# The shared rotary key of an encoder layer: which operand stands still in TensorE and which one streams

## The reference, cut to what matters

```python
h = rms_norm(x, norm_mix_g[l])
z = h @ w_in[l]
u_conv, c_q, c_kv, k_pe, gate_logits = jnp.split(z, IN_SPLITS, axis=-1)   # k_pe: 64 columns
...
k_pe = apply_rope(k_pe, cos, sin)
k_full = jnp.concatenate(
    [k_nope, jnp.broadcast_to(k_pe[:, :, None, :], (B, S, MLA_HEADS, QK_ROPE))], axis=-1)
```

## Time and profile before

| | |
|---|---|
| median of the runs | 1637.82 us |
| the profiled execution, whole | 1639.63 us |
| its span, first to last instruction | 1637.8 us |
| TensorE busy with matmuls | 1624.3 us (99%), 7612 matmuls |
| TensorE busy with weight loads | 1360.0 us (83%) |
| VectorE / ScalarE / GpSimd busy | 1088.9 / 811.2 / 98.2 us |
| mean granted TensorE clock | 0.998 of 2.4 GHz |

### The profile page before, as it was taken

How to read it: one execution, slowest core, us unless ns; L and a number is a source line. 1 busy time by engine, 2 the same in 40 slices (tenths; PEclk the granted TensorE clock), 3 DMA queues, 4 the chain that set the end, 5 groups by cost and what they waited for, 6 DMA issues and landing times.

```text
span 1637.8 us, 22071 instructions
## 1 busy us (share of the span) xinstructions
PE 1624.3 (99%) x7612; PEld 1360.0 (83%) x7612; DVE 1088.9 (66%) x1480; ACT 811.2 (50%) x1062; POOL 98.2 (6%) x187
## 2 busy tenths in 40 slices
PE   9999999999999999999999999999999999999998
PEld 7888888888888888888889888888888888888886
DVE  5588888888888998656556655555555555545554
ACT  6444456555555556744445644334443444334443
POOL 6500010211111000000000000000000000000000
PEclk9999999999999999999999999999999999999999
DMA  7766655555555665557554566566656665566654
GB/s 242 204 191 187 186 160 162 173 170 175 180 166 160 219 201 184 183 190 249 199 186 150 166 182 190 192 193 182 192 189 192 193 182 186 193 191 186 190 188 138
DMA packets 160992, 304.78 MB, mean 186 GB/s; under 512 B 11657, under 2 KB 19969, under 8 KB 160513
## 3 DMA queue, kind: packets, MB, share of 16 engines
q1 hardware_dynamic: 159552, 299.41, 59.7%
q0 software_dynamic: 1056, 3.46, 0.6%
q10 hardware_dynamic: 320, 1.06, 0.2%
HBM read 301.78 MB, written 2.10 MB: 186 GB/s over the span
## 4 chain that ended last, share of the span: by engine, by line
PE 97%; ACT 1%; DVE 1%; DMA 0%; issue 0%; SPq 0%
PE ps L1328 30%; PE ps L1330 30%; PE ps L1329 30%; PE ps L1341 2%; PE ps L1512 1%; PE ps L1511 1%; PE ps L1601 0%; PE ps L1599 0%; PE ps L1600 0%; ACT hconv L759 0%; PE ps L1528 0%; DMA x_in<-in_x_dram 0%; PE ps L1522 0%; PE ps L1365 0%; PE ps L1692 0%
## 5 line engine op out<-in xcount | busy, mean ns | idle before, releaser
L895 DVE TENSOR_TENSOR wlo<-raw,whi 128x1024 fp32r<-128x1024 f32 x560 | 686.0, 1228 | 406.6 <-ACT whi L544 402.0
L544 ACT ACTIVATE whi<-raw 128x1024 fp32r<-128x1024 f32 x560 | 591.7, 1060 | 567.4 <-PE ps L1330 555.9
L1328 PE MATMUL ps<-whi,a_hi 128*128 128x512 f32 x1212 | 478.0, 394 | 0.0
L1330 PE MATMUL ps<-whi,a_lo 128*128 128x512 f32 x1212 | 472.3, 390 | 0.0
L1329 PE MATMUL ps<-wlo,a_hi 128*128 128x512 f32 x1212 | 471.9, 389 | 0.0
L1328 PE MATMUL ps<-whi,c_hi 128*128 128x512 f32 x752 | 293.8, 391 | 0.0
L1330 PE MATMUL ps<-whi,c_lo 128*128 128x512 f32 x752 | 292.7, 389 | 0.0
L1329 PE MATMUL ps<-wlo,c_hi 128*128 128x512 f32 x752 | 292.6, 389 | 0.0
L1330 PEld LDWEIGHTS ps<-whi,a_lo 128*128 128x128 f32 x1212 | 227.5, 188 | 47.8
L1329 PEld LDWEIGHTS ps<-wlo,a_hi 128*128 128x128 f32 x1212 | 227.7, 188 | 45.7
L1328 PEld LDWEIGHTS ps<-whi,a_hi 128*128 128x128 f32 x1212 | 227.6, 188 | 45.7 <-DVE wlo L895 0.2
(11 more groups left out here) (255 smaller groups left out, 1169.3 us busy)
## 6 DMA issues: line engine op xcount, KB each, us to landing
raw<-in_w_ff_dram SPq DMA_DIRECT2D x256, 512.0 KB, 4.0
raw<-in_w_in_dram SPq DMA_DIRECT2D x144, 512.0 KB, 3.7
raw<-in_w_mla_out_dram SPq DMA_DIRECT2D x32, 512.0 KB, 4.4
raw<-in_w_conv_out_dram SPq DMA_DIRECT2D x32, 512.0 KB, 4.2
raw<-in_w_out_dram SPq DMA_DIRECT2D x32, 512.0 KB, 4.6
raw<-in_w_ukv_dram SPq DMA_DIRECT2D x16, 512.0 KB, 3.7
raw<-in_w_xkv_dram SPq DMA_DIRECT2D x16, 512.0 KB, 4.1
raw<-in_w_uq_dram SPq DMA_DIRECT2D x16, 384.0 KB, 3.7
```

The source lines that it names most:

```text
L544: act.activation(whi[:, s, :], raw[:, s, :], ACT.Copy).then_inc(hi_ready, 1)
L895: dve.tensor_tensor(wlo[:, s, :], raw[:, s, :], whi[:, s, :].bitcast(F32), ALU.subtract).then_inc(lo_ready, 1)
L1328: pe.matmul(sum_, x_hi[:, k0 + k, tok], w_hi, start=(first and k == 0), stop=False)
L1330: mm = pe.matmul(sum_, x_lo[:, k0 + k, tok], w_hi, start=False, stop=(last and k == kts - 1))
```

## The change

The 128-token blocks of the activations stand, and the 64 weight columns move. There are 16 blocks of channels x 2 token halves x 3 products = 96 matmuls. Token rows come out at once, 128 tokens x 64 channels in bank 4 for the first half of the tokens and in bank 5 for the second. ScalarE reads `kpe_row` directly from these banks, with the same scale. The copy into `kpe_sum`, the two transposes, the tile and the semaphore `kpe_out` are gone, and the wait for `vec_ready` stands ahead of the matmuls.

```diff
# ScalarE
                 if k == 0:
                     act.wait_ge(used, U_KPE + 1)
-                    act.activation(kpe_sum[:], ps[0:ROPE, 4, 0:SEQ], ACT.Copy).then_inc(kpe_out, 1)
-                if k == 1:
-                    act.wait_ge(kpe_turned, 1)
                     for t in range(TT):
-                        last = act.activation(kpe_row[:, t, :], ps[:, 5, ROPE * t:ROPE * (t + 1)], ACT.Copy, scale=rs_x[:, t:t + 1])
+                        last = act.activation(kpe_row[:, t, :], ps[:, 4 + t, 0:ROPE], ACT.Copy, scale=rs_x[:, t:t + 1])
                     last.then_inc(kpe_ready, 1)
...
                 if k == 5:
-                    act.wait_ge(kpe_turned, 2)
+                    act.wait_ge(kpe_turned, 1)
# TensorE
             pe.wait_ge(lo_ready, U_KPE + 1)
+            pe.wait_ge(vec_ready, 2)
             s = U_KPE % RING
             for k in range(KT):
                 w_hi, w_lo = (w[:, s, ROPE * k:ROPE * (k + 1)] for w in (whi, wlo))
-                pe.matmul(ps[0:ROPE, 4, 0:SEQ], w_hi, a_hi[:, k, :], start=(k == 0), stop=False)
-                pe.matmul(ps[0:ROPE, 4, 0:SEQ], w_lo, a_hi[:, k, :], start=False, stop=False)
-                mm = pe.matmul(ps[0:ROPE, 4, 0:SEQ], w_hi, a_lo[:, k, :], start=False, stop=(k == KT - 1))
+                for t in range(TT):
+                    to, tok = ps[:, 4 + t, 0:ROPE], slice(P * t, P * (t + 1))
+                    pe.matmul(to, a_hi[:, k, tok], w_hi, start=(k == 0), stop=False)
+                    pe.matmul(to, a_hi[:, k, tok], w_lo, start=False, stop=False)
+                    mm = pe.matmul(to, a_lo[:, k, tok], w_hi, start=False, stop=(k == KT - 1))
             mm.then_inc(used, 1)
             for k in range(UPC):
                 unit(U_CKV + k, 0, a_hi, a_lo, 2 * k, 0, k == 0, k == UPC - 1)
-                if k == 0:
-                    pe.wait_ge(kpe_out, 1)
-                    pe.wait_ge(vec_ready, 2)
-                    for t in range(TT):
-                        tr = pe.transpose(ps[:, 5, ROPE * t:ROPE * (t + 1)], kpe_sum[:, P * t:P * (t + 1)], ident[0:ROPE, 0:ROPE])
-                    tr.then_inc(kpe_turned, 1)
```

More of the change, by code:

```diff
@@ L233, in build @@
         mask = at(o + 27648, "mask", [P, SW])
-        kpe_sum = at(o + 20480, "kpe_sum", [ROPE, SEQ])
         kpe_row = at(o + 29184, "kpe_row", [P, TT, ROPE])
@@ L313, in build @@
         ln_root, ln_scaled, silu_done, st_hi, st_lo = (sem(n) for n in ("ln_root", "ln_scaled", "silu_done", "st_hi", "st_lo"))
-        kpe_out, kpe_ready, kpe_prod, kpe_rotated, kpe_turned, kpeT_ready = (sem(n) for n in ("kpe_out", "kpe_ready", "kpe_prod", "kpe_rotated", "kpe_turned", "kpeT_ready"))
+        kpe_ready, kpe_prod, kpe_rotated, kpe_turned, kpeT_ready = (sem(n) for n in ("kpe_ready", "kpe_prod", "kpe_rotated", "kpe_turned", "kpeT_ready"))
         q_ready, qn_ready, kv_ready, q_prod, q_rotated = (sem(n) for n in ("q_ready", "qn_ready", "kv_ready", "q_prod", "q_rotated"))
```

## The result

The changed kernel takes 1652.99 us, the median of 4 runs (1652.17 to 1654.65), beside 1638.2 us for the kernel before (1637.47 to 1638.91, now 4 runs, one more than the 1637.82 rests on). The ratio is 1.0089 with a 95% interval of 1.0077 to 1.0101: slower by 14.8 us, where +5.1 (1642.9 us) was forecast. The profiled execution took 1652.17 us, 12.5 more than the one before.

A forecast was written before the change was run, and what follows sets the result against it. TensorE's own work was taken to bound the kernel (busy 1624.3 of 1637.8 us). +5.6 us for the rotary matmuls and -0.46 for the transposes gave +5.1, so 1642.9 us; own range 1642.0 to 1643.8, overall 1641.0 to 1652.5.

The forecast's parts named there:

- The likeliest case: Rotary matmuls load-bound at full clock, stretch 10.6 to 11.5 us, kernel about 5.1 us slower; chance 0.53.
- 96 x 0.115 = 11.0 us: Rotary stretch on TensorE: 96 new matmuls at 0.115 us each, against 5.45 us before, so +5.6 us.
- Rival A: Clock falls in the stretch of short rotary matmuls: +10.8 to +14.4 us, 1648.6 to 1652.2; chance 0.26.
- higher case: Clock falls 3.6 us into the rotary stretch, 65 matmuls at 0.23 us follow: +14.4 us, 1652.2.
- The row behind its 0.23 us: Trace row giving (2.50 - 0.42)/9 = 0.23 us for a 128-column load and pass, taken as the lower-clock price.
- the one stretch that lost its clock: Kernel start: PE busy 1.17 of 3.60 us, after which the clock stood at 0.50 from 8.95 to 12.40.
- The load as the bound: Rotary matmuls: each needs its own 128-column load, which sets the pace at 0.11 to 0.12 us.
- Rival B: Rotary matmuls take two passes, or load and stream in turn, 0.22 us each: +15.2 us, 1653.0; chance 0.07.
- Rival C: Rotary matmuls' load as quick as a transpose's, 0.06 us each: -0.1 us, 1637.7, no change; chance 0.09.
- -0.46 us for the transposes: Two transposes behind the rotary matmuls go: 0.92 us between two matmul starts becomes 0.46.
- No cost for the other engines: ScalarE's two 0.50 us copies instead of one of 0.36 are covered; GpSimd's rotation stays hidden; VectorE and ScalarE simply stand.
- No wait behind them gets longer or shorter: After the rotary stretch: TensorE's later waits stay the same, every later instruction about 5.1 us later.

The follow-up runs named there:

- wide128: Changed kernel with each of the 96 matmuls streaming 128 weight columns instead of 64 (last block 64), same loads; 1644.12 us, ratio 1.0034.
- spread4: Changed kernel's 96 matmuls in four parts of 24 with a full c_kv unit between parts; 1644.38 us, ratio 1.0035.
- wide256: Changed kernel with up to 256 weight columns streamed per matmul (last three blocks 192, 128, 64); 1645.55 us, ratio 1.0039.
- stack: Kernel before, with high and low weights standing side by side: 32 matmuls instead of 48, two identity matmuls replacing the transposes; 1637.28 us, ratio 0.9989.
- halves: Changed kernel's 96 matmuls in two parts of 48 with one full c_kv unit between; 1652.27 us, ratio 1.0081.

## Why the prediction was wrong

- **The likeliest case was the wrong one.** The step that failed is "96 x 0.115 = 11.0 us", with "granted clock 1.00" in the stretch. The pace was right as long as the clock was (0.1115 us in the changed kernel, 0.1113 in wide128); 56 of the 96 matmuls ran at 0.2134, and the 96 took 16.33 us. The forecast sum also had no term for the full unit behind them, which lost 2.5 us more.
- **Rival A, at 0.26, is what happened**, and its price was near: 65 matmuls at 0.23 us were forecast, 56 at 0.2134 came; 1.7 us of loss behind the stretch were forecast, 2.5 came. Its higher case, 1652.2, lies 0.8 us under the median. That closeness is in part luck: at the place itself its +14.4 us stand beside 12.85 read, since the matmuls at the lower clock were fewer and quicker than priced (11.95 us instead of 15.0), while the later fall and the dearer full unit took back 1.6; what the median has beyond the place brings the two together. The row behind its 0.23 us lies where the profile records no lower clock; the 0.2134 measured at 0.50 bears the price out all the same. The range ended at 1652.5, 0.5 short.
- **Where I misread the rows.** I set the one stretch that lost its clock (1.17 of 3.60 us busy) against one that kept it (2.04 of 3.40) and asked whether matmuls always under way count as busy. PE reads 100% busy in the whole stretch of short matmuls, and the clock fell all the same. wide128 and spread4 show what the busy row hides: with loads and pace equal, the width of the stream or full units between decide. The change cut the stream to a quarter per 0.11 us; that number opened rival A, but the case in which the clock falls got 0.26 and the other 0.53.
- **The load as the bound: right for the new shape.** 0.111 with 64 or 128 moving columns. The row it was taken from was misread: at 256 moving columns (0.12 us) the load alone does not set the pace, as wide256 shows, so that row was a bound for the new shape and not its price. The 0.115 taken between the rows is 0.0035 us too high, 0.3 us in all. Rival B (two passes, 0.22 us) is out: 96 matmuls, one instruction each. The 0.21 us that the stretch shows is the lower clock. Rival C (a load as quick as a transpose's) is out at full clock by the same 0.111; why the transposes of the earlier trace rows go at 0.06 with loads of 128 columns was not tested.
- **-0.46 us for the transposes: right.** In the changed kernel the lower clock hides it, but the sum by places fits to 0.1 us (10.9 + 2.5 - 0.46 beside the 12.85 read). In wide128, at full clock and without the transposes, the same two matmuls start 0.45 us apart (226.50 and 226.95), where they had started 0.92 apart.
- **No cost for the other engines: right** for the place; 11 us of standing still cost nothing beyond TensorE's own.
- **"No wait behind them gets longer or shorter": wrong by up to about a microsecond.** In every kernel here with more matmuls than before, TensorE waits for issue once in the MLP (0.2 to 0.8 us); neither the kernel before nor stack, which has fewer, shows it. That it comes from where the longer program's code lies is argued, not shown.

## What to carry to other kernels

Price a short matmul by the columns of its load and check what it streams meanwhile: swapping the operands here halved the stream and doubled the loads twice over. A stretch in which PE is 100% busy can lose half the clock when it streams as sparsely as here, 64 columns in each 0.11 us without a break (it fell after 4.4 us), and the full matmuls behind it pay too; break such a stretch up with dense work, widen the stream, or let one load serve more products. Look for it in the clock row, not in the busy row.

## What the runs showed of the hardware

- Widening 90 streams by 64 columns that nobody reads made the kernel 9 us faster (1644.12 beside 1652.99; +5.5 beside +14.8, each against the kernel before on its own chip): the clock stayed at 1.00.
- At the granted clock of 0.50 the short matmuls' pace went from 0.1115 to 0.2134 us and a full unit's from 2.73 to 5.20.
- In the changed kernel the clock came back at 233.60, 5.1 us after full matmuls had begun again. In halves it came back 5.8 us after the unit between had begun (220.01 to 225.82), when the next short matmuls were already under way.
- With 128 columns standing, an fp32r matmul takes 0.111 us with 64 or 128 moving columns and 0.120 with 256; with 64 standing it takes 0.058 with 64 moving and 0.1135 with 256.
- Where it falls is not fixed: 4.4 us after the first short matmul in the changed kernel, 3.0 in halves, each read from one profile. Whether it moves from run to run is not shown; in halves the quickest run spent less time at 0.50 than the others (mean clock 0.995 beside 0.993).
